# Four of twelve modulation parts are made behind the first block's attention, around the m11 and out projections

## What is computed

```python
sc = jax.nn.silu(c)
sc_ctx = jax.nn.silu(c_ctx)
for layer in range(DEPTH_2):
    mod = sc @ ada_w[layer] + ada_b[layer]
    shift, scale, gate = jnp.split(mod[:, None, :], 3, axis=-1)
    mod_c = sc_ctx @ ada_w[layer] + ada_b[layer]
    shift_c, scale_c, gate_c = jnp.split(mod_c, 3, axis=-1)
    u = rms_norm_2(h, norm_g[layer]) * (1 + scale) + shift
```

## Time and profile before

| | before |
|---|---|
| median of 3 runs | 1176.54 us (1175.92 to 1177.77) |
| profiled execution | 1176.58 us, its span 1174.7 us |
| PE busy | 1082.5 us (92%) |
| PEld, DVE, ACT, POOL busy | 708.3, 474.4, 414.9, 194.9 us |
| mean granted clock of PE | 0.992 |
| DMA | 333.59 MB, mean 284 GB/s |

### The profile page before, as it was taken

The page is one execution under the profiler, slowest core; times in us unless marked ns, Lnnn a source line. Parts: engine busy times, 40 slices in busy tenths (PEclk is TensorE's granted clock), DMA queues, the critical chain, the costliest instruction groups (busy, mean ns, idle before and its releaser), DMA issues. The chain is left out here.

```text
span 1174.7 us, 17461 instructions
## 1 busy us (share of the span) xinstructions
PE 1082.5 (92%) x6884; PEld 708.3 (60%) x6884; DVE 474.4 (40%) x1046; ACT 414.9 (35%) x792; POOL 194.9 (17%) x272
## 2 busy tenths in 40 slices
PE   8999888999988979798988899998999999999997
PEld 7887545557522424344544235356887886999775
DVE  4566456445300001123433012106776545454655
ACT  5445443343110101014332002004445654444873
POOL 2002553000000000003120000004431233001550
PEclk9999999999999999999999999999999999999999
DMA  9856598556699999999999999996521414655300
GB/s 362 314 166 251 213 353 310 231 221 279 236 426 431 429 430 425 430 431 430 429 430 427 425 428 428 428 410 205 168 73 55 158 47 129 216 185 187 103 19 36
DMA packets 55721, 333.59 MB, mean 284 GB/s; under 512 B 5840, under 2 KB 6096, under 8 KB 43216
## 3 DMA queue, kind: packets, MB, share of 16 engines
q1 hardware_dynamic: 55632, 332.39, 72.1%
HBM read 331.32 MB, written 1.05 MB: 283 GB/s over the span
## 5 line engine op out<-in xcount | busy, mean ns | idle before, releaser
L490 ACT ACTIVATE ab<-w 128x1024 fp32r<-128x1024 f32 (+2 forms) x117 | 122.0, 1049 | 181.5 <-PE ps L506 174.5
L500 DVE TENSOR_TENSOR ab<-w,ab 128x1024 fp32r<-128x1024 f32 (+2 forms) x101 | 124.0, 1233 | 127.5 <-ACT ab L490 127.3
L2583 PE MATMUL ps<-w,vT 128*32 128x512 f32 x1024 | 123.4, 606 | 34.2 <-DMA w<-in_w_gate 25.1
L506 PE MATMUL ps<-ab,uA 128*128 128x512 f32 x320 | 101.3, 398 | 3.1 <-ACT gr L1597 1.3
L2583 PEld LDWEIGHTS ps<-w,vT 128*32 128x32 f32 x1024 | 28.7, 110 | 112.9 <-issue 75.3
L506 PE MATMUL ps<-UA,ab 128*128 128x256 f32 x512 | 94.4, 285 | 1.3 <-DVE ab L500 1.3
L506 PE MATMUL ps<-ab,UA 128*128 128x512 f32 (+1 forms) x288 | 87.9, 386 | 0.0
L506 PEld LDWEIGHTS ps<-UA,ab 128*128 128x128 f32 x512 | 80.3, 192 | 2.0 <-DVE ab L500 1.5
L506 PE MATMUL ps<-UB,ab 128*128 128x256 f32 x256 | 72.4, 283 | 0.0
L2633 PE MATMUL ps<-w,bT 128*32 128x512 f32 x512 | 61.7, 606 | 11.2 <-DMA w<-in_w_down 5.7
L506 PEld LDWEIGHTS ps<-ab,uA 128*128 128x128 f32 x320 | 59.8, 190 | 17.7 <-issue 3.9
(11 more groups left out here) (554 smaller groups left out, 1865.2 us busy)
## 6 DMA issues: line engine op xcount, KB each, us to landing
w<-in_w_up SPq DMA_DIRECT2D x32, 2048.0 KB, 18.6
w<-in_w_gate SPq DMA_DIRECT2D x32, 2048.0 KB, 17.4
w<-in_w_down SPq DMA_DIRECT2D x32, 2048.0 KB, 18.3
w<-in_w_ada SPq DMA_DIRECT2D x48, 512.0 KB, 7.9
w<-in_w_c SPq DMA_DIRECT2D x42, 512.0 KB, 4.4
w<-in_w_m SPq DMA_DIRECT2D x16, 512.0 KB, 4.6
w<-in_ab_out_w SPq DMA_DIRECT2D x10, 512.0 KB, 6.7
w<-in_w_out SPq DMA_DIRECT2D x8, 512.0 KB, 12.0
```

Source lines behind the costliest of these rows:

```text
L490: e.activation(sp.a(j), w.v, ACT.Copy).then_inc(sp.whole, 1)
L500: e.tensor_tensor(sp.b(j), w.v, sp.a(j).bitcast(F32), ALU.subtract).then_inc(sp.parts[j % NAB], 1)
L506: ins = e.matmul(out_, l[x], r[y], start=start and n == 0, stop=stop and n == 2)
L2583: ins = e.matmul(t.ps[o, :], ve[:, p % 2, 2 * c + k, o], w.v[:, 2 * a + k, :], start=c + k == 0, stop=c + k == 4)
```

## The change

Eight parts (`SOON`: layer 0's six and layer 1's first two) stay in the attention stage, with six steps each in place of four, again 48 steps. The other four (`LATE_ADA`) are given to PE in six pieces: `ada12` before the turning of `go`; its transposes between the two matmul groups of `pgla0`; `ada13` after the second quarter of `m11`; its transposes after the fourth; `ada14` and `ada15` after `pgla1`; their transposes after `mxT`. ACT's and DVE's pieces stand in their programs where the diff shows, and seven of the idle groups' matmul calls become two. The four late parts are evacuated into `bP[:, 2]` and `bT[:, 2]` and take PSUM banks of the ring of eight. The loads of their 16 tiles move with PE's requests. `cnorm` waits for layer 0's modulation alone.

```diff
+        SOON, LATE_ADA = [(0, c) for c in range(6)] + [(1, 0), (1, 1)], [(1, c) for c in range(2, 6)]
+        ADA_REST = 2
...
         def pe_modulations(e, ring):
...
+            for l, c in SOON:
+                pe_ada(e, ring, l, c)
+                yield
+                yield
+                pe_ada_sum(e, ring, l, c)
+                yield
+                yield
+                for _ in range(ADA_REST):
                     yield
...
+            def late_modulations():
+                for l, c in LATE_ADA[0:2]:
+                    pe_ada(e, ALL, l, c)
+                    yield
+                    pe_ada_sum(e, ALL, l, c)
+                    yield
+                for l, c in LATE_ADA[2:]:
+                    pe_ada(e, ALL, l, c)
+                yield
+                for l, c in LATE_ADA[2:]:
+                    pe_ada_sum(e, ALL, l, c)
+                yield
+
+            late = late_modulations()
             for c in range(2):
                 if c == 1:
-                    pe_lin(e, S1, "m11", uA, uB, 512, range(2))
+                    for quarter, _ in enumerate(pe_lin_steps(e, S1, "m11", uA, uB, 512, range(2))):
+                        if quarter % 2 == 1:
+                            next(late)
                 for n, x, p in (("nsa_o", ynT, "pnsa"), ("ogT", ogT, "pgla")):
                     if c == 0 and n == "ogT":
+                        next(late)
                         e.wait_ge(go_done, 2)
...
                             project(n, x, p, c, i, i == 0, done)
-            pe_idle_next(e, ALL, 4)
+                        if c + i == 0 and n == "ogT":
+                            next(late)
+            next(late)
+            pe_idle_next(e, ALL, 1)
             e.wait_ge(mix_done, 4)
...
-            pe_idle_next(e, ALL, 3)
+            next(late)
+            pe_idle_next(e, ALL, 1)
...
+            act_splits(e, S1, "m11.2")
+            act_ada(e, *LATE_ADA[0])
+            act_splits(e, S1, "m11.3")
+            act_ada(e, *LATE_ADA[1])
             act_lin(e, S1, "m11", [xsm[:, i, 1, :] for i in range(2)], ACT.Sigmoid, scaled=True)
             act_squares(e, [h[:, 2, :], h[:, 3, :]], 2, bT[:, 0:2, :].rearrange("p a n -> p (a n)"))
             act_context_norm(e)
+            for l, c in LATE_ADA[2:]:
+                act_ada(e, l, c)
...
                     e.wait_ge(gates, 4)
+                    dve_ada(e, *LATE_ADA[0])
                     dve_lin(e, S1, "m11")
+                    dve_ada(e, *LATE_ADA[1])
...
                 dve_lin(e, S1, f"out{c}")
+                if c == 0:
+                    for l, x in LATE_ADA[2:]:
+                        dve_ada(e, l, x)
+                    dve_modulated(e, 1)
...
-            e.wait_ge(modulated, 4)
+            e.wait_ge(modulated, 2)
```

More of the change, by code:

```diff
@@ L1002, in build @@
         WARM_ZERO, ANGLES, ABS_A = 1, 2, 3
-        def pe_modulations(e, ring):
[L1005 to L1019, removed]
-                    yield
[L1021 to L1030, removed]
@@ L1032, in act_modulations @@
-        def act_modulations(e):
[L1033 to L1040, removed]
+        SOON, LATE_ADA = [(0, c) for c in range(6)] + [(1, 0), (1, 1)], [(1, c) for c in range(2, 6)]
@@ new lines, in build, with ada_part, pe_ada @@
+        ADA_REST = 2
+        def ada_part(n):
+            if n < len(SOON):
+                return rt[:, 2 * (n % 2):2 * (n % 2) + 2, :].rearrange("p a b -> p (a b)")
+            return (bP, bT)[n % 2][:, 2, :]
+        def pe_ada(e, ring, l, c):
+            t = bank.take(ring, "ada")
+            free(e, t)
+            if (l, c) == (0, 0):
+                e.wait_ge(act_made, COND)
+            for k in range(8):
+                w = W[f"ada{l}{c}.{k // 2}"]
+                if k % 2 == 0:
+                    e.wait_ge(w.full, w.n)
+                o = slice(32 * (k % 4), 32 * (k % 4) + 32)
+                ins = e.matmul(t.ps[o, :], scT[:, k, :], w.v[:, k % 2, :], start=k < 4, stop=k > 3)
+            ins.then_inc(t.full, 1)
+            for m in range(4):
+                W.release(f"ada{l}{c}.{m}", t.full, t.n)
@@ new lines, in pe_ada_sum @@
+        def pe_ada_sum(e, ring, l, c):
+            n = 6 * l + c
+            t, part = bank["ada"][n], ada_part(n)
+            e.wait_ge(t.evac, t.n)
+            g = bank.take(ring, "ada_sum")
+            free(e, g)
+            for j in range(4):
+                ins = e.transpose(g.ps[:, j * 128:(j + 1) * 128], part[:, j * 128:(j + 1) * 128], ident)
+            ins.then_inc(g.full, 1)
+        def pe_modulations(e, ring):
+            for l, c in SOON:
[6 more added lines that the diff above has]
+                for _ in range(ADA_REST):
+                    yield
@@ new lines, in act_ada @@
+        def act_ada(e, l, c):
+            n = 6 * l + c
+            t = bank["ada"][n]
+            e.wait_ge(t.full, t.n)
+            if (l, c) in LATE_ADA[2:]:
+                g = bank["ada_sum"][n - 2]
+                e.wait_ge(g.full, g.n)
+            e.activation(ada_part(n), t.ps[:, :], ACT.Copy).then_inc(t.evac, 1)
+        def act_modulations(e):
+            for l, c in SOON:
+                yield
[3 more added lines that the diff above has]
+                yield
+                for _ in range(ADA_REST):
@@ L1041, in act_modulations, with dve_ada @@
                     yield
         modulated = sem("modulated")
-        def dve_modulations(e):
-            for l in range(2):
-                for c in range(6):
-                    yield
[L1049 to L1061, removed]
+        def dve_ada(e, l, c):
+            t = bank["ada_sum"][6 * l + c]
+            e.wait_ge(t.full, t.n)
+            o = mod[:, l, 4 * c:4 * c + 4, :]
+            e.tensor_reduce(o, t.ps[:, :].rearrange("p (j g x) -> p j x g", j=4, g=4)[:, :, 0:2, :], X, ALU.add).then_inc(t.evac, 1)
+            e.wait_ge(t.evac, t.n)
+            V_.did(e.tensor_tensor(o, o, bc(S("adab")[:, 24 * l + 4 * c:24 * l + 4 * c + 4], 2, 2), ALU.add))
@@ new lines, in dve_modulated @@
+        def dve_modulated(e, l):
+            V_.after()
+            for wh in range(2):
+                e.scalar_tensor_tensor(out=Amod[:, l, wh, :], in0=mod[:, l, 8:16, wh], scalar=1.0, in1=S("ng0" if l == 0 else "ng1"),
+                                       op0=ALU.add, op1=ALU.mult).then_inc(modulated, 1)
+        def dve_modulations(e):
+            for l, c in SOON:
+                yield
+                yield
+                yield
+                dve_ada(e, l, c)
+                yield
+                for _ in range(ADA_REST):
+                    yield
+                if (l, c) == (0, 5):
+                    dve_modulated(e, 0)
@@ L1063, in idle_modulations @@
         def idle_modulations():
-            for _ in range(48):
+            for _ in range((4 + ADA_REST) * len(SOON)):
                 yield
```

## The result

| | before | after |
|---|---|---|
| median | 1176.59 us (4 runs, 1175.92 to 1177.77) | 1199.32 us (4 runs, 1198.61 to 1200.85) |
| profiled execution, its span | 1176.58, 1174.7 us | 1200.85, 1199.0 us |
| PE busy | 1082.5 us | 1094.0 us |
| mean granted clock of PE | 0.992 | 0.976 |

The time is 1.0189 of that before, with a 95% interval of 1.0174 to 1.0204. It is slower, as forecast, but by 22.7 us where 8.15 were forecast, and outside the range.

The account below looks back on a forecast made before the run. PE was taken to bound the kernel nearly everywhere before the load-bound experts. Terms -10.0 + 4.6 + 10.7 + 1.4 + 1.45 = +8.15 us on 1176.58 gave 1184.7 us, range 1178.5 to 1190.5.

Parts of the forecast that it names:

- I take them to nearly double: Attention stage: PE's waits on POOL's scaled keys grow from 4.2 to 7.9 us, leaving 10.0 us won.
- Rival (b): Attention stage: the chain of POOL and ACT bounds it, winning 5 us or less; 1189.5 us, chance 14%.
- if the attention stage shrinks by less than 5 us: Attention stage: a sign that the forecast is wrong; it expected about 69 to 70 us with eight parts.
- Twice 2.31 us, in full: +4.6: Behind the attention stage: `ada12` and `ada13` cost PE their full matmuls and transposes, with no gap to hide them.
- Their evacuations come in time: Behind `pnsa0`: ACT evacuates `ada12` by about 6 us after its end, before PE asks at some 7.6 us.
- The stall before cnorm: Between `pnsa1` and `cnorm`: out0.2 waits for `pnsa1`'s slot, ACT's split and rows come late, PE stalls: +10.7 us.
- it decides from where the stall is under 4 us: Before `cnorm`: the faster rival holds below that stall, so if out0.2's load were issued 7 us before `pnsa1` ends.
- rival (a): Before `cnorm`: out0.2's load doesn't hold the chain, so no stall or clock cost; 1172.6 us, chance 9%.
- The clock behind the stall: Behind the stall of 11 us: PE's clock falls once, +1.4 us, from nothing to 2.8.
- parts 14 and 15: Around `mxT`: `ada14` and `ada15` overfill PE's gap after `pgla1`, +1.45 us; their transposes cost nothing.
- rival (d): `cnorm` and `pgla1`: the clock stays low, up to 4.4 us in place of 1.4; 1187.7 us, chance 10%.
- rival (c): Experts: the delay vanishes there since loads set the end, no change; 1176.6 us, chance 5%.

Follow-up runs that it names:

- filler runs: Changed kernel plus two idle matmul calls, or one, before each of eight waits for POOL's scaled keys: 1195.88 us and 1195.64 us.
- b_bank: Changed kernel, but `ada12` takes its PSUM bank from a separate one-bank ring, so the ring of eight isn't advanced: 1192.94 us.
- d_behind: Changed kernel, but ACT splits out0.0 to out0.2 only behind the context rows, and DVE's lower parts move later too: 1187.04 us.
- a_split_later: Changed kernel, but ACT and DVE split only out0.0 and out0.1 before going on with m11, out0.2 later: 1192.41 us.
- dbc: d_behind plus the other PSUM bank for `ada12` and two idle matmul calls before each wait for POOL's keys: 1178.47 us.
- four_best: d_behind with one idle call before each wait for POOL's keys, `ada12` behind the turning of `go`, `ada12`, `ada13`, `ada15` on a separate bank: 1175.63 us.
- two_best: Changed kernel with only `ada14` and `ada15` late, splits as in d_behind, one idle call before each keys wait, `ada15` on a separate bank: 1177.06 us.

## Why the prediction was wrong

The working held in three terms of five, and the sum failed by the other two: 8.75 us in the attention stage and 5.8 us in the parts behind it.

**The attention stage (forecast -10.0, measured -1.25).** The step that failed is "I take them to nearly double", and with it the missing price of the clock. The work that leaves PE was right in size, and the waits for sums went. But the waits for POOL's keys grew from 4.2 to 9.0 us, not to 7.9, and 1.5 us for `qT` came that no term had. And the value taken, like its least gain of 5.3, rested on a PE that keeps its speed: the granted clock fell to 0.50 four times in the stage. The windows put the miss at 6.3 us of busy time (3.0 less where 9.24 of work left) and 2.6 of waits (1.8 more where 0.8 less was forecast). The filler runs cut it another way. At full clock, with one call of filler, the stage is 6.5 us shorter than before, not 10 (82.87 against 76.38): some 3.5 us are waits that a steady clock doesn't take away. The other 5.4 us (81.74 against 76.38) are what the clock costs in the end. (Both splits are of the stage's length, which shrank by 1.13 us; the other 0.12 of the -1.25 is an earlier start.) The forecast put the clock only behind the long stall. Rival (b), the chain of POOL and ACT and a gain of 5 us or less, came true in its gain, and so did the sign "if the attention stage shrinks by less than 5 us"; but of the two causes it had one, and at full clock the stage gains more than its 5 us.

**Parts 12 and 13 (forecast +4.6, measured +10.41).** The step that failed is "Twice 2.31 us, in full: +4.6", which put every new wait at nothing. The reason given for it, "Their evacuations come in time", held as far as it went: ACT had evacuated `ada12` at 220.17 us, 5.75 behind the end of `pnsa0`, where P+6 was forecast. But it asked only when their own results leave PSUM, not which bank they push the next projection onto. The 5.8 us above are that bank (3.8 of wait) and the clock behind it (2.0). b_bank, which changed only the bank, had neither, and its second stage was 5.45 us shorter, the rest within 0.4 us of the forecast.

**The stall before cnorm (forecast +10.7, measured +10.59).** Right in place, cause and size, each of its terms within 0.15 us; d_behind removed it by moving the splits. The Trainium skill's advice ("DMA: Bandwidth & Descriptors", section "Rules for kernel authors") to issue a load early and wait for it late holds here: in d_behind ACT does its other work before it waits, and the stall is gone. What the forecast missed is that the loads of out0.0 and out0.1 were late too. They stand in the queue behind `ada15`'s tiles, which wait for the slots of `ada13`'s; the forecast counted these slots, and asked the question only for out0.2. That cost nothing in this kernel, and made "it decides from where the stall is under 4 us" in rival (a) too simple: a_split_later removed out0.2 from the chain and still had a stall of 5.19 us.

**The clock behind the stall (forecast +1.4, measured +1.86)** and **parts 14 and 15 (forecast +1.45, measured +1.29).** Right; the first also rules out rival (d), which had up to 4.4 us for it. So was the claim that the delay reaches the end whole, which rules out rival (c): 22.9 us at the first expert matmul, 22.7 at the end of the experts.

The range failed because its upper bounds were added for the named terms alone: even all high, they gave 1192.4 us. Both misses are costs of the same kind, of an in-order engine that is shifted against others: a bank, and the idle time that brings the clock down.

## What to carry to other kernels

When an instruction that takes a slot or a bank is inserted into a ring, count the ring for everything behind it, and ask of each new neighbour when the old use is released: here that was one weight slot (10.6 us), the slots of the tiles ahead in the queue (5.19 us of stall once the first was out of the way) and one PSUM bank (5.8 us with the clock). Work that stands before another engine's result is cover; price its removal as less gain than its own length, and read the granted clock where it stood. And repair the late loads before adding up gains from others, as three repairs that each gave 3.4 to 6.9 us gave 9.9 together until the last one was found.

## What was not expected of the hardware

The granted clock fell to 0.50 in the attention stage with PE busy for 68.14 of 81.74 us and no wait longer than 2.03 us there; one idle call before each of eight waits kept it at 1.00 and made the stage 3.9 to 5.4 us shorter. All four profiled kernels with eight parts and no filler had such falls in the stage, and none of the six with filler had. It also fell between 283 and 292 us in the profiled executions of dbc, four_best and two_best (283 to 289 us in the last), with PE busy for at least 0.9 of every microsecond from 270 us on in the last; the kernel before ran the same matmuls at 1.00. The rule in the Trainium skill, "TensorE: Matmul & The Clock Gate", section "HAM oscillation — how this bites in real kernels", ties such falls to single long waits of PE. The traces agree behind the waits of 4.90 and 11.00 us. They don't show such a wait ahead of the falls in the attention stage, where it was the filler that kept them away, nor ahead of those at 283 to 292 us. What brings the latter about stays open.
